# Two conv buffers and later gate matmuls in a recurrent branch, and modulation sums moved to another stage

## The chip, the cores and the metric

The kernel runs on one core of one Trainium2 chip. The metric is the device time of one execution in microseconds. A core has TensorE (PE, matrix multiplies into the PSUM banks), VectorE (DVE), ScalarE (ACT), GpSimd (POOL) and SyncE (SP, which here only issues transfers). Each engine runs its own list of instructions in order, and they wait for each other through semaphores.

## What is computed

Two blocks of a network on 1024 tokens of width 1024, in float32. The first block is a mixer of attention and a gated linear recurrence; the second takes its shift, scale and gate vectors ("modulation") from a small vector `c`. The parts that matter here:

```
proj = h @ w_in ; q, k, v, g_attn, x_lru, g_lru = split(proj)
xc = causal_depthwise_conv(x_lru, conv_w, conv_b)      # 4 taps
r  = sigmoid(xc_block @ w_r + b_r)                     # 8 blocks of 128
gi = sigmoid(xc_block @ w_i + b_i)
a  = exp(-8 * r * softplus(-lam))
h_t = a_t * h_{t-1} + sqrt(1 - a_t**2) * gi_t * xc_t
y_lru = h_t * silu(g_lru)
x = x + rmsnorm(concat(y_attn, y_lru) @ w_out)
...
mod = silu(c) @ w_ada_2 + b_ada_2                      # 6 x 1024 values, used from the second block on
```

## The kernel before

Activations lie feature-major: a tile is 128 features by 1024 tokens, and eight tiles make the width. Weights come as 255 slabs of 1024 x 128 (512 KB), in the order of their use, in two slots. For each slab SyncE issues one load (`load_slab`, L242) as soon as GpSimd has split the slab two places ahead. GpSimd splits it into a high part (L225, a cast) and a low part (L227, a subtraction), once TensorE has finished the slab two places ahead. `project` (L207 to L209) then multiplies it: for each of two chunks of 512 tokens, 8 inner tiles times 3 matmuls (high x high, high x low, low x high), 24 matmuls into one PSUM bank; chunk 0 goes to `proj_bank0`, chunk 1 to `proj_bank1`. A bank can be written again when ScalarE or VectorE has read it.

**Recurrent branch** (`lru_stage`, about 50 to 308 us of the trace, eight blocks n of 128 features, a loop on every engine). Each block has two slabs, one for x and one for the gate branch.
- TensorE: slab x, chunk 0 of the gate slab, six one-column matmuls that add up the modulation of the block before (`columns`, L499, shown as x12 since the profile counts the passes of a float32 matmul), chunk 1, and then, after a wait for the convolution, the four gate matmuls (L514, shown as x8).
- ScalarE: two silus (L542), two sigmoids (L546, L547), exp and tanh (L549, L550), the copy of the next block's x chunk 0 (L537), the square root (L554), the copy of chunk 1. Between kinds of functions it loads a table.
- VectorE: a copy of the block's gate weights (L598), the convolution (L599 and three times L602), the modulation's six values (L581), six of eight accumulations of modulation weights (L589, L591: `acc = w_ada[kt] * cond[kt] + acc`, 128 x 768), three steps of the recurrence (L609, L610, L612), the last two accumulations, the product with the root (L615), the scan (L617) and the product with silu (L620).
- SyncE: the loads of the next two slabs, and then eight loads of modulation weights (L490, 384 KB each, two buffers), each of which waits until VectorE has used the one two places ahead.

The convolution's output `lru_conv` is one buffer, read by the gate matmuls and by L612. The copy of the next x goes out only when the convolution has read the last.

**Attention** (about 308 to 1052 us): its first matmuls run at once, but its ScalarE part begins when all engines have ended the branch (`begin` waits for `stage_ended`). Its first copy of a chunk is L819.

**Output projection** (`out_project_stage`, about 1052 to 1230 us). VectorE first makes eight low parts of y (L1028). TensorE projects the last slabs of tile 0; then a loop of seven rounds f projects tile f+1, two slabs each. ScalarE squares and copies each tile (L1019, L1020), and VectorE adds the squares up (L1033), one instruction for each tile. The next stage (the norm, L277) begins when all engines have ended this one. SyncE's queue from slab 18 on is `rest_of_slabs`, a plain loop over pairs of slabs.

## Time and profile before

| | us |
|---|---|
| median of 3 runs | 3740.36 |
| lowest and highest run | 3737.33 and 3741.08 |
| span of the profiled execution | 3738.0 |
| TensorE busy | 3485.4 (93%) |
| VectorE busy | 1433.6 (38%) |
| ScalarE busy | 829.6 (22%) |
| GpSimd busy | 949.5 (25%) |

The profile gives no other time of the profiled execution than its span; it lies 2.4 us below the median run. Times in a timeline are counted from the start of the span. The busy time of a matmul overlaps with the next one's, so the distance from start to start is what a matmul costs. The granted clock of TensorE is given as a share of 2.4 GHz; 0.5 is its lower level.

### The profile page before, as it was taken

Reading aid. Unit: us, or ns where it says so; the run is one execution under the profiler, and the core shown is the slowest. Engines: PE = TensorE matmul, PEld = TensorE weight load, DVE = VectorE, ACT = ScalarE, POOL = GpSimd, SP = SyncE. Lnnn points to the kernel's source line nnn. Section 1 sums busy time; section 2 is a strip of 40 time slices with the busy share of each in tenths; the row PEclk is TensorE's granted clock in tenths of the full one; section 3 lists DMA queues with packets and bytes.
Section 4 is the critical chain, followed back from the end, with each engine's and each line's share of the span. In section 5 each row is a group of like instructions: output and inputs, shape, how many; then the busy total and the mean of one; then the engine's idle time right before and its main releaser. Section 6 shows DMA issues by size and latency. Waiting matters only on the chain.

```text
span 3738.0 us, 42270 instructions
## 1 busy us (share of the span) xinstructions
PE 3485.4 (93%) x16158; PEld 2816.6 (75%) x16158; DVE 1433.6 (38%) x1753; ACT 829.6 (22%) x1308; POOL 949.5 (25%) x514
## 2 busy tenths in 40 slices
PE   6888999999889798899999999979999989999999
PEld 5666777777668386677888888868878768888887
DVE  6774444444520557642012222321621543223231
ACT  3332232333320232232122222221110011101010
POOL 2222111111023131112322212224323323333332
PEclk9898999999889799989999999989999989999999
DMA  3432000000001211111121212232111211111112
GB/s 137 126 115 87 23 29 23 23 29 23 12 28 50 107 45 51 51 57 40 50 91 54 66 48 71 52 113 63 50 39 50 86 33 51 45 50 46 49 50 73
DMA packets 83681, 213.93 MB, mean 57 GB/s; under 512 B 7024, under 2 KB 33264, under 8 KB 83456
## 3 DMA queue, kind: packets, MB, share of 16 engines
q1 hardware_dynamic: 48176, 167.27, 14.2%
q10 hardware_dynamic: 35408, 45.24, 3.9%
q8 instruction: 77, 1.26, 0.1%
q14 instruction: 20, 0.16, 0.0%
HBM read 193.44 MB, written 19.04 MB: 57 GB/s over the span
## 4 chain that ended last, share of the span: by engine, by line
PE 81%; DVE 12%; ACT 2%; issue 2%; DMA 1%; PEld 0%; ACTq 0%; DVEq 0%; PEldq 0%; POOL 0%; SPq 0%; POOLq 0%
PE proj_bank L207 20%; PE proj_bank L209 19%; PE proj_bank L208 19%; PE aux_banks L719 3%; PE aux_banks L207 2%; PE aux_banks L209 2%; PE aux_banks L208 2%; PE aux_banks L785 1%; PE aux_banks L729 1%; PE aux_banks L1702 1%; PE aux_banks L514 1%; DVE lru_conv L602 1%; PE aux_banks L1385 1%; PE aux_banks L722 1%; DVE ada_acc L591 1%
## 5 line engine op out<-in xcount | busy, mean ns | idle before, releaser
L207 PE MATMUL proj_bank<-h_hi,slab_hi 128*128 128x512 f32 x2816 | 1131.5, 402 | 36.3 <-DVE h_lo L372 9.1
L208 PE MATMUL proj_bank<-h_lo,slab_hi 128*128 128x512 f32 x2816 | 1111.0, 395 | 0.0
L209 PE MATMUL proj_bank<-h_hi,slab_lo 128*128 128x512 f32 x2816 | 1110.8, 394 | 0.0
L225 POOL CAST slab_hi<-slab_raw 128x1024 fp32r<-128x1024 f32 x255 | 274.3, 1076 | 2745.9 <-PE proj_bank L209 2343.9
L227 POOL TENSOR_TENSOR slab_lo<-slab_raw,slab_hi 128x1024 fp32r<-128x1024 f32 x255 | 675.1, 2647 | 20.4
L207 PEld LDWEIGHTS proj_bank<-h_hi,slab_hi 128*128 128x128 f32 x2816 | 538.6, 191 | 160.1 <-issue 20.2
L209 PEld LDWEIGHTS proj_bank<-h_hi,slab_lo 128*128 128x128 f32 x2816 | 537.6, 191 | 116.3
L208 PEld LDWEIGHTS proj_bank<-h_lo,slab_hi 128*128 128x128 f32 x2816 | 538.7, 191 | 109.8 <-issue 2.2
L207 PE MATMUL proj_bank<-ffn_hi,slab_hi 128*128 128x512 f32 x512 | 199.2, 389 | 0.0
L208 PE MATMUL proj_bank<-ffn_lo,slab_hi 128*128 128x512 f32 x512 | 199.2, 389 | 0.0
L209 PE MATMUL proj_bank<-ffn_hi,slab_lo 128*128 128x512 f32 x512 | 199.2, 389 | 0.0
L2257 ACT ACTIVATE ffn_relu_squared<-proj_bank 128x512 f32<-128x512 f32 x64 | 38.4, 599 | 538.2 <-PE proj_bank L209 438.5
L2285 DVE SCALAR_TENSOR_TENSOR x<-proj_bank,mod,x 128x512 f32<-128x512 f32 x64 | 48.1, 751 | 276.2 <-PE proj_bank L209 276.2
L828 ACT ACTIVATE att_p<-aux_banks,small 128x256 f32<-128x256 f32 (+7 forms) x128 | 93.7, 737 | 215.2 <-DVE small L891 214.9
L2275 DVE SCALAR_TENSOR_TENSOR ffn_relu_squared<-ffn_relu_squared 128x1024 f32<-128x1024 f32 x32 | 51.8, 1619 | 219.3 <-ACT ffn_relu_squared L2257 219.3
L719 PE MATMUL aux_banks<-att_k,att_q 64*128 64x512 f32 (+3 forms) x320 | 132.2, 519 | 0.0
L889 DVE TENSOR_REDUCE small<-aux_banks 128x1 f32<-128x256 f32 (+7 forms) x128 | 96.1, 755 | 75.1 <-PE aux_banks L723 74.4
L207 PE MATMUL proj_bank<-y_hi,slab_hi 128*128 128x512 f32 x256 | 104.5, 408 | 10.5 <-DVE y_lo L1028 4.4
L208 PEld LDWEIGHTS proj_bank<-ffn_lo,slab_hi 128*128 128x128 f32 x512 | 96.1, 188 | 20.0
L209 PEld LDWEIGHTS proj_bank<-ffn_hi,slab_lo 128*128 128x128 f32 x512 | 96.1, 188 | 20.0
L207 PEld LDWEIGHTS proj_bank<-ffn_hi,slab_hi 128*128 128x128 f32 x512 | 96.1, 188 | 19.9
L208 PE MATMUL proj_bank<-y_lo,slab_hi 128*128 128x512 f32 x256 | 103.0, 402 | 0.0
(329 smaller groups left out, 4243.3 us busy)
## 6 DMA issues: line engine op xcount, KB each, us to landing
slab_raw<-wts SPq DMA_DIRECT2D x255, 512.0 KB, 3.5
ada_w<-ada_w SPq DMA_DIRECT2D x64, 384.0 KB, 3.1
ssd_decay_rows<-decay_sums ACTq DMA_DIRECT2D x16, 512.0 KB, 4.1
dil_rows<-dilated_out ACTq DMA_DIRECT2D x12, 520.0 KB, 8.0
x_first<-xT SPq DMA_DIRECT2D x4, 1024.0 KB, 9.5
x_again<-xT ACTq DMA_DIRECT2D x4, 1024.0 KB, 10.5
x_kept<-x ACTq DMA_DIRECT2D x8, 512.0 KB, 3.8
mix_kept<-ssd_mix ACTq DMA_DIRECT2D x8, 512.0 KB, 6.4
```

The costliest lines, as they stand in the source:

```text
L207: pe.matmul(bank, k.whi[:, slot, wk, :], hi[:, xk, cols], start=first and a == 0, stop=False)
L208: pe.matmul(bank, k.whi[:, slot, wk, :], lo[:, xk, cols], start=False, stop=False)
L209: mm = pe.matmul(bank, k.wlo[:, slot, wk, :], hi[:, xk, cols], start=False, stop=last and a == len(ks) - 1)
L225: pool.tensor_copy(k.whi[:, slot], k.raw[:, slot]).then_inc(k.s_hi, 1)
L227: pool.tensor_tensor(k.wlo[:, slot], k.raw[:, slot], k.whi[:, slot].bitcast(F32), ALU.subtract).then_inc(k.s_split, 1)
L514: mm = pe.matmul(k.aux[:, 2 * i + c, :], gw[:, i, :], xc[:, c * HALF:(c + 1) * HALF], start=True, stop=True)
L719: pe.matmul(score[:, 2 * c + a // HALF, 0:n], q, kt[rows, par, a:a + n], start=True, stop=True)
L828: act.activation(p[:, c, 0:keys], flat[:, c, 0:keys], ACT.Exp, bias=nmax[:, c:c + 1], scale=SCALE, accum_out=total[:, c:c + 1]).then_inc(s ...
L889: ins = dve.tensor_reduce(mx[:, c:c + 1], flat[:, c, 0:keys], AX, ALU.max)
L2257: act.activation(act2[:, f % 2, c * HALF:(c + 1) * HALF], k.bank[c][:], ACT.Copy).then_inc(s_read, 1)
L2275: dve.scalar_tensor_tensor(act2[:, f % 2], act2[:, f % 2], 0.0, act2[:, f % 2], ALU.max, ALU.mult).then_inc(s_sq, 1)
L2285: dve.scalar_tensor_tensor(xt, k.bank[c][:], k.mod[:, 40 + f:41 + f], xt, ALU.mult, ALU.add).then_inc(s_x2, 1)
```

## The change

- The branch is written out (no loops). `lru_conv` gets two buffers. On TensorE the gate matmuls of block n-1 stand between the x slab and the gate slab of block n. On ScalarE the copies of x(n) come first, then sigmoids, exp and tanh of n-1, the silus of n, the root of n-1. On VectorE the convolution of n comes ahead of the recurrence of n-1. The copy of the gate weights is gone; TensorE reads them where they were loaded.
- The modulation leaves the branch. Its loads, accumulations and columns are now in the output projection, one group of eight loads for each of the eight tiles: VectorE accumulates ahead of adding up the squares, and TensorE's `columns(f)` stand between the two slabs of round f, the last ones behind the loop. SyncE's queue has each group behind a pair of slabs (slabs 50 and 51 for the first), and the first loads wait until VectorE has begun the stage.

```diff
-def lru_stage(k, block, wts, gate_w, ada_w):
+def lru_stage(k, block, gate_w):
...
+    xc = k.at("lru_conv", k.W + 4.25, [P, 2, T])
...
     def _(pe):
...
-        with pe.Fori(0, LRU_BLOCKS) as n:
+        for n in range(LRU_BLOCKS):
             for s in range(2):
                 for c in range(2):
-                    pe.wait_ge(s_evac, n * 4 + (2 * s + c + 1))
-                    project(k, pe, n * 2 + (LRU_0 + s), s, c, k.bank[c][:], k.hhi, k.hlo, ready=h_ready)
-                    if s == 1 and c == 0:
-                        columns(n)
-            pe.wait_ge(s_conv, n + 2)
-            pe.wait_ge(s_sig, n + 1)
-            for i in range(2):
-                for c in range(2):
-                    mm = pe.matmul(k.aux[:, 2 * i + c, :], gw[:, i, :], xc[:, c * HALF:(c + 1) * HALF], start=True, stop=True)
-            mm.then_inc(s_gates, 1)
+                    pe.wait_ge(s_evac, 4 * n + 2 * s + c + 1)
+                    project(k, pe, LRU_0 + 2 * n + s, s, c, k.bank[c][:], k.hhi, k.hlo, ready=h_ready if n == 0 else None)
+                if s == 0 and n:
+                    gates(n - 1)
+        gates(LAST)
...
     def _(act):
...
+        for n in range(LRU_BLOCKS):
+            for c in range(2):
+                x_in(n, c)
+            if n:
+                decays(n - 1)
+            silu(n)
+            if n:
+                root(n - 1)
+        decays(LAST)
+        root(LAST)
...
     def _(dve):
...
+        for n in range(LRU_BLOCKS):
+            conv(n)
+            if n:
+                recurrence(n - 1)
+        recurrence(LAST)
...
 def out_project_stage(k, block):
...
                     project(k, pe, f * 2 + (OUT1_0 + 2 + s), s, c, k.bank[c][:], k.yhi, k.ylo,
                             [(i, i + KT * s) for i in range(KT)], s == 0, s == 1)
+                    if s == 0 and c == 1:
+                        columns(f)
+        columns(GROUPS - 1)
...
         with dve.Fori(0, KT) as f:
+            modulation(f)
             dve.wait_ge(s_added, f + 1)
             dve.wait_ge(s_evac, f * 2 + 4)
             dve.tensor_tensor(k.ssum, k.ssum, sq, ALU.add).then_inc(s_added, 1)
+            columns(f)
...
-def rest_of_slabs(k, block, wts):
+def rest_of_slabs(k, block, wts, ada_w):
...
+        with sp.Fori(0, KT) as n:
+            pair(n + first)
+            for kt in range(KT):
+                sp.wait_ge(k.s_ada_used, n * KT + (kt + 1))
+                sp.dma_start(k.adaw[:, kt % 2], ada_w[ds(n, 1), kt].rearrange("a p m -> (a p) m")).then_inc(k.s_ada[kt % 2], 16)
```

TensorE in the recurrent branch. Before, the end of a block of the loop (L207 to L209 are the gate slab, L514 the gate matmuls):

```order
L209 MATMUL proj_bank<-h_hi,slab_lo 128x512
L510 REGISTER_ALU
L511 REGISTER_ALU [waits lru_conv_made]
L514 MATMUL aux_banks<-lru_conv,gate_w 128x512 [waits lru_sigmoids]
L514 MATMUL aux_banks<-lru_conv,gate_w 128x512 x3
L503 REGISTER_ALU
L503 COMPARE_AND_BRANCH
```

TensorE after the change, the first gate matmuls (L206 to L208 are the x slab of block 1 ahead of them and its gate slab behind them, L492 the gate matmuls of block 0):

```order
L206 MATMUL proj_bank<-h_hi,slab_hi 128x512
L207 MATMUL proj_bank<-h_lo,slab_hi 128x512
L208 MATMUL proj_bank<-h_hi,slab_lo 128x512
L492 MATMUL aux_banks<-lru_conv,gate_w_all 128x512 [waits lru_conv_made,gate_w_loaded]
L492 MATMUL aux_banks<-lru_conv,gate_w_all 128x512 x3
L206 MATMUL proj_bank<-h_hi,slab_hi 128x512 [waits slab_split,lru_evacuated]
```

The gate matmuls ended their own block; they now stand one slab later, inside the next one.

ScalarE in the recurrent branch. Before, a block of the loop (L542 are the silus of n, L537 the copies of x of n+1):

```order
L542 ACT_TABLE_LOAD
L542 ACTIVATE y<-proj_bank 128x512
L541 REGISTER_ALU
L542 ISA [waits chunk_projected]
L542 ACTIVATE y<-proj_bank 128x512
L544 REGISTER_ALU
L546 ISA [waits lru_y_made,lru_gates]
L546 ACT_TABLE_LOAD
L546 ACTIVATE lru_r<-aux_banks,params 128x1024
```

ScalarE at the same place after the change (L524 are the copies of x of n, L535 to L539 sigmoids, exp and tanh of n-1, L529 the silus of n, L543 the root of n-1):

```order
L524 ACTIVATE lru_x<-proj_bank 128x512 [waits chunk_projected,lru_conv_made] x2
L535 ACT_TABLE_LOAD [waits lru_y_made]
L535 ACTIVATE lru_r<-aux_banks,params 128x1024 [waits lru_gates]
L536 ACTIVATE lru_i<-aux_banks,params 128x1024
L538 ACT_TABLE_LOAD
L538 ACTIVATE lru_a<-lru_r,small 128x1024 [waits lru_sigmoids]
L539 ACTIVATE lru_u<-lru_r,small 128x1024
L529 ACT_TABLE_LOAD
L529 ACTIVATE y<-proj_bank 128x512 [waits chunk_projected] x2
L543 ACT_TABLE_LOAD
L543 ACTIVATE lru_r<-lru_u 128x1024 [waits lru_m2]
```

The silus stood ahead of the sigmoids of their own block; they now stand behind the four activations of the block before, and the wait for the gates stands behind the table load.

VectorE in the output projection. Before, the loop holds one instruction for each tile:

```order
L1028 TENSOR_TENSOR y_lo<-y,y_hi 128x1024 [waits y_high] x7
L1029 MEMSET out_sum 128x1024
L1030 UNCONDITIONAL_BRANCH
L1030 ISA
L1032 ISA [waits out1_added]
L1033 TENSOR_TENSOR out_sum<-out_sum,out_squared 128x1024 [waits out1_evacuated]
```

VectorE, the end of the same loop after the change (L1020 is the last of eight accumulations, L1034 the sum of the squares, L1027 the six values that it reads from TensorE's columns):

```order
L1020 SCALAR_TENSOR_TENSOR ada_acc<-ada_w,small,ada_acc 128x768 [waits ada_loaded_1,ada_used]
L1022 REGISTER_ALU
L1032 REGISTER_ALU [waits ada_used]
L1033 ISA [waits out1_added]
L1034 TENSOR_TENSOR out_sum<-out_sum,out_squared 128x1024 [waits out1_evacuated]
L1027 ISA [waits ada_columns]
L1027 TENSOR_TENSOR mod<-aux_banks,params 128x6
```

Eight accumulations have come ahead of the sum, and the read of the columns behind it.

## Rows read from the trace of the kernel before

**Rows 1.** Table of stretches: length, engines' busy us, PEclk, DMA share, GB/s.

```profile
core 0: us, PE busy (x) PEld busy (x) DVE busy (x) ACT busy (x) POOL busy (x), PEclk, DMA share, GB/s
200.00:250.00 50.00, 43.74 (x162) 31.39 (x163) 35.69 (x29) 20.92 (x21) 11.28 (x5) 0.86 0.42 127
...
1150.00:1227.00 77.00, 77.00 (x341) 63.79 (x340) 3.68 (x3) 7.60 (x14) 26.89 (x14) 1.00 0.15 48
```

**Rows 2.** Table of waits, TensorE, 60 to 330 us: total, times, longest.

```profile
PE aux_banks L514 <- DVE lru_conv L602: 33.3, 7, 5.7
```

**Rows 3.** Timeline of TensorE in the branch: start, us, line, tile [idle before].

```profile
67.03 3.59 PE L514 MATMUL aux_banks<-lru_conv,gate_w 128*128 128x512 f32 x8
...
70.69 0.40 PE L208 MATMUL proj_bank<-h_lo,slab_hi 128*128 128x512 f32 x1
...
148.40 0.39 PE L207 MATMUL proj_bank<-h_hi,slab_hi 128*128 128x512 f32 x1
...
155.20 1.39 PE L499 MATMUL aux_banks<-small,ada_acc 128*128 128x1 f32 x12
...
156.78 0.40 PE L208 MATMUL proj_bank<-h_lo,slab_hi 128*128 128x512 f32 x1
...
167.90 5.99 PE L514 MATMUL aux_banks<-lru_conv,gate_w 128*128 128x512 f32 x8 [5.69 <-DVE lru_conv L602]
...
308.15 0.47 PE L207 MATMUL proj_bank<-h_hi,slab_hi 128*128 128x512 f32 x1 [0.41 <-PEq L701]
```

**Rows 4.** Groups by line, 30 to 330 us: busy us, mean ns | idle before.

```profile
L514 PE MATMUL aux_banks<-lru_conv,gate_w 128*128 128x512 f32 x64 | 45.1, 870 | 33.3 <-DVE lru_conv L602 33.3
L225 POOL CAST slab_hi<-slab_raw 128x1024 fp32r<-128x1024 f32 x17 | 23.2, 1362 | 222.1 <-DMA slab_raw<-wts 118.1 <-PE proj_bank L209 104.0
...
L542 ACT ACT_TABLE_LOAD x8 | 10.3, 1283 | 34.5 <-PE proj_bank L209 34.4
...
L542 ACT ACTIVATE y<-proj_bank 128x512 f32 (+1 forms) x16 | 9.6, 598 | 44.3 <-PE proj_bank L209 44.3
```

**Rows 5.** Timeline of ScalarE, VectorE and TensorE around the branch's last block.

```profile
190.88 2.29 DVE L617 TENSOR_TENSOR_SCAN lru_u<-lru_a,lru_i 128x1024 f32<-128x1024 f32 x1
...
307.79 1.12 ACT L546 ACTIVATE lru_r<-aux_banks,params 128x1024 f32<-128x1024 f32 x1 [9.06 <-PE aux_banks L514]
...
312.28 1.14 ACT L550 ACTIVATE lru_u<-lru_r,small 128x1024 f32<-128x1024 f32 x1
...
316.23 1.06 ACT L554 ACTIVATE lru_r<-lru_u 128x1024 f32<-128x1024 f32 x1 [1.51 <-DVE lru_u L610]
...
319.57 1.23 DVE L615 TENSOR_TENSOR lru_i<-lru_i,lru_r 128x1024 f32<-128x1024 f32 x1
...
324.10 2.95 DVE L620 TENSOR_TENSOR y<-lru_u,y 128x1024 f32 x1 [0.26 <-DVE lru_u L617]
...
328.25 0.79 PE L207 MATMUL proj_bank<-h_hi,slab_hi 128*128 128x512 f32 x1 [6.86 <-ACT att_q L819]
```

**Rows 6.** Instructions on one tile, GpSimd, 60 to 310 us: ns min/median/max.

```profile
L227 POOL TENSOR_TENSOR slab_lo<-slab_raw,slab_hi x15: 2950/3194/4249, 68.5 to 298.1; 128x1024 fp32r<-128x1024 f32 x15
```

**Rows 7.** Timeline of the output projection: its loop's start and its end.

```profile
1070.78 2.34 POOL L227 TENSOR_TENSOR slab_lo<-slab_raw,slab_hi 128x1024 fp32r<-128x1024 f32 x1
...
1073.18 0.50 PE L207 MATMUL proj_bank<-y_hi,slab_hi 128*128 128x512 f32 x1 [3.69 <-POOL slab_lo L227]
...
1229.89 2.87 PE L277 MATMUL aux_banks<-small,out_sum 128*128 128x1 f32 x16 [2.48 <-DVEq L191]
```

**Rows 8.** Timeline of VectorE, one block's accumulations of the modulation.

```profile
167.76 0.60 DVE L589 TENSOR_SCALAR ada_acc<-ada_w,small 128x768 f32<-128x768 f32 x1
...
171.36 1.02 DVE L591 SCALAR_TENSOR_TENSOR ada_acc<-ada_w,small,ada_acc 128x768 f32<-128x768 f32 x1 [1.94 <-DMA ada_w<-ada_w]
...
175.68 1.02 DVE L591 SCALAR_TENSOR_TENSOR ada_acc<-ada_w,small,ada_acc 128x768 f32<-128x768 f32 x1 [1.32 <-DMA ada_w<-ada_w]
...
177.66 1.02 DVE L591 SCALAR_TENSOR_TENSOR ada_acc<-ada_w,small,ada_acc 128x768 f32<-128x768 f32 x1 [0.96 <-DMA ada_w<-ada_w]
```

**Rows 9.** Instructions on the tile of the modulation weights, whole span: their landing.

```profile
DMA to landing us min/median/max: 2.8/3.1/6.5
```

More of the change, by code:

```diff
@@ L479, in lru_stage @@
     s_lam = k.sem("lambda_summed")
-    k.banks_read = (s_evac, 2 * LRU_SLABS + 2)
-    EV, AD = 2, 6
-    @block.sync
-    def _(sp):
-        with sp.Fori(0, LRU_BLOCKS) as n:
-            for s in range(2):
-                load_slab(k, sp, wts, n * 2 + (2 + s), s, True)
-            for kt in range(KT):
-                sp.wait_ge(s_ada_used, n * KT + (kt + 2))
-                sp.dma_start(adaw[:, kt % 2], ada_w[ds(n, 1), kt].rearrange("a p m -> (a p) m")).then_inc(s_ada[kt % 2], 16)
+    EV = 2
@@ L492, in _, with gates @@
+    k.banks_read = (s_evac, 2 * LRU_SLABS + EV)
+    LAST = LRU_BLOCKS - 1
     @block.tensor
     def _(pe):
-        def columns(n):
-            pe.wait_ge(s_ada_used, n * KT + 3)
-            pe.wait_ge(s_col, n * 2 + 1)
-            for j in range(AD):
-                mm = pe.matmul(k.aux[:, 4, j:j + 1], acc[:, j * P:(j + 1) * P], k.ones, start=True, stop=True)
-            mm.then_inc(s_col, 1)
+        def gates(n):
+            if n == 0:
+                pe.wait_ge(s_gw, 16)
+            pe.wait_ge(s_conv, n + 1)
+            if n:
+                pe.wait_ge(s_sig, n)
+            for i in range(2):
+                for c in range(2):
+                    mm = pe.matmul(k.aux[:, 2 * i + c, :], gw[:, n, i, :], xc[:, n % 2, c * HALF:(c + 1) * HALF], start=True, stop=True)
+            mm.then_inc(s_gates, 1)
@@ L516, in _ @@
+        gates(LAST)
         end(k, pe)
         def last_sums():
-            columns(LRU_BLOCKS)
             pe.wait_ge(k.s_vec, 1)
@@ L546, in rest @@
[L546 to L552 removed]
+            if n:
+                act.wait_ge(s_y, n)
@@ L990, in out_project_stage, with columns @@
     k.ssum = k.at("out1_sum", k.W + 36, [P, T])
-    s_evac, s_added = k.sem("out1_evacuated"), k.sem("out1_added")
+    adaw, acc = k.adaw, k.at("ada_acc", k.W + 46, [P, ADA_COLS])
+    s_evac, s_added, s_col = k.sem("out1_evacuated"), k.sem("out1_added"), k.sem("ada_columns")
+    AD = ADA_COLS // P
+    GROUPS = KT
     @block.tensor
     def _(pe):
+        def columns(n):
+            pe.wait_ge(k.s_ada_used, n * KT + (KT + 2))
+            for j in range(AD):
+                mm = pe.matmul(k.aux[:, 4, j:j + 1], acc[:, j * P:(j + 1) * P], k.ones, start=True, stop=True)
+            mm.then_inc(s_col, 1)
         begin(k, pe)
```

132 lines of the change are left out of this document (58 added, 74 removed).

## The prediction

> **What bounds the kernel now.** I looked first at the table of stretches, to see which engine fills each stage. In the output projection TensorE is busy for the whole stretch and its granted clock is full; in the recurrent branch it is busy for 43.7 of 50 us with a granted clock of 0.86, while VectorE is busy for 35.7 us [rows 1]. So the branch is the one of the two touched stages in which TensorE is kept waiting, and the table of waits says by whom: from 60 to 330 us TensorE waited 33.3 us, in seven pieces, for the last step of the convolution (L602) [rows 2]. The timeline shows the shape of a block: the gate matmuls (L514) stand right behind the second slab, so they wait for a chain that begins only when the recurrence of the block before has left VectorE. They then run long: 5.99 us behind a wait, against 3.59 us in block 0, where there was none [rows 3]. That is the granted clock: behind the idle time the matmuls go at the lower of the two levels, 1.2 GHz, for a while.
>
> The Trainium skill says the same, in "TensorE: Matmul & The Clock Gate", section "HAM oscillation — how this bites in real kernels": a wait in each round lets the clock fall, and each round pays for it again. The trace agrees (5.99 against 3.59 us); a sum of the waits alone would leave out some 16 us, which is the first rival below.
>
> **Recurrent branch, removed and moved.** Unit prices first. 30 projection matmuls stand between the starts at 148.40 and 155.20, so one takes 0.2267 us and a slab (48 of them) 10.88 us. The gate matmuls at full clock: 67.03 to 70.69 holds them and one projection matmul, so 3.66 - 0.23 = 3.43 us. The columns of the modulation (L499): 155.20 to 156.78 holds them and one matmul, so 1.35 us [rows 3]. Now the stretch from the first gates (67.03) to the first matmul of the attention (308.15): 241.1 us. After the change, block 0 reaches that point without columns, at 67.03 - 1.35 = 65.68, and what is left are 14 slabs and 8 sets of gates: 14 x 10.88 + 8 x 3.43 = 179.8 us, up to 245.4. That is **62.7 us less**. As a cross-check, by parts: 33.3 us of waits, 45.1 - 8 x 3.59 = 16.4 us of slow gates [rows 2 to 4], 8 x 1.35 = 10.8 us of columns, and 2.2 us of slow matmuls behind the gates.
>
> This holds only if nothing else sets the pace of 25.2 us a block. ScalarE has the tightest place: silu of chunk 0 now stands behind the four activations of the block before, and it frees the bank that the next x slab needs 10.9 us after the gates end. From the last block, written out in straight code already: the sigmoids begin at 307.79, the tanh ends at 313.42, 5.6 us; a table load 1.28 and the silu 0.6 make 7.5 us [rows 4, 5]. 3.3 us are left. VectorE: the convolution needs only its own block's x, which is there 24 us before the gates ask for the result. The recurrence: silu of chunk 1 ends 11.5 us after the gates, table load and root 2.3, and 5.0 to 7.5 us for product, scan and y (worked out below), so 19 to 21.5 us, before the next x is complete at 22. GpSimd needs 1.4 + 3.2 = 4.6 us a slab, 5.6 with the longest subtraction here (4.25), of 10.9 [rows 4, 6]. SyncE has only slabs left in its queue, so these come earlier than before.
>
> **Start of the attention.** ScalarE may take the attention's first chunk only when VectorE has ended the branch. TensorE waits 6.9 us for that (L819). Before: sigmoids at 307.79, root ends at 317.29, 9.5 us; then two accumulations (L591) stand in front of the product at 319.57; y ends at 327.05, TensorE goes on at 328.25 [rows 5]. The accumulations go. Product, scan and y took 4.53 + 2.95 = 7.5 us here, beside GpSimd; with the short scan of 2.29 and a y as long as the product they take 1.23 + 2.29 + 0.26 + 1.23 = 5.0. So 9.5 + 5.0 to 7.5 + 1.2 = 15.7 to 18.2 us; I take 17.1, for GpSimd's subtraction falls into this place as before. TensorE resumes at 245.4 + 17.1 = 262.5, against 328.25. With the 62.7 us that makes **65.8 us**, 64.6 to 67.1.
>
> **Output projection, added.** The loads, sums and columns of the modulation come here, one group a tile. Three terms:
> - Columns: 7 in the loop x 1.35 = **9.4 us** on TensorE, which has no free time there [rows 1]; 8.8 if the slow matmul behind them is spared.
> - The first slab of the loop: TensorE waits 3.69 us for GpSimd's split (L227, 2.34 us, VectorE mostly idle) [rows 7]. VectorE now accumulates at that time, and in the branch, where it did, the subtraction took 3.19 us at the median and 4.25 at most [rows 6]: **0.9 us**, 0 to 1.9. The Trainium skill ("GPSIMD Engine Reference", section "Specifications") says that GpSimd shares its SBUF interfaces with VectorE and contends with instructions that read two SBUF inputs, as the accumulation does; the medians agree.
> - The end. A group in the branch went 167.76 (first piece), 171.36 (third), 175.68 (fifth), 177.66 (sixth) [rows 8]. Carried on at 4.32 us a pair: 3.60 + 2 x 4.32 + 1.98 + 1.02 = 15.2 us. Within the loop a group may take from one tile's columns to the next's, 21.8 + 1.35 = 23.1 us, of which 1.65 go for columns and their read: 15.2 < 21.4, so 6 us are left and TensorE doesn't wait. The last group has only the second slab beside it. Counted from the middle of the last round it ends at 1.65 + 15.2 = 16.9 us, while the matmuls end at 12.2; then come the columns at the lower clock (up to 2.5 us), their read and the end of the stage, so the next stage begins at 18.9 to 20.0. Before, it began 10.9 + 2.5 us after that point [rows 7]; with the seventh columns already counted, 14.75. **4.7 us**, 4.1 to 5.3.
>
> SyncE's queue: slabs now stand behind eight loads of the modulation that each wait for VectorE. The last of them is issued some 11 us into the group, so a slab's load is issued up to 9 us later than now. But the split can't begin before the slab two places ahead has been projected, another 10 us later, and the longest landing of a modulation load is 6.5 us [rows 9]; so this costs nothing. The first eight loads wait until VectorE begins the stage, and the first group (from about 1064 to 1079) is through before its columns are wanted at 1086.
>
> **Sum.** 65.8 - 9.4 - 0.9 - 4.7 = 50.8 us. The profiled execution spans 3738.0 us, 2.4 less than the median of 3740.4; against the median: 3740.4 - 50.8 = **3689.6**. Its own range goes from 3685 to 3693 by the bounds above, and some 4 us more on either side for clock levels that fall differently in the later stages: 3681 to 3697.
>
> **Rivals.**
> 1. The gates stay slow: TensorE's clock doesn't hold, although it doesn't wait. Then only waits and columns go, 16.4 us less: 3706. For it: the gates carry twice the time of a projection matmul, and only block 0 shows eight of them at the full clock. Against: 77 us of unbroken work at 1.00 [rows 1]. Chance 0.05.
> 2. ScalarE or VectorE paces the branch. If the 3.3 us in front of silu are used up and 3 us more, each of seven blocks loses 3 us: +21, 3711. For it: y and the convolution stretch to 3 us beside GpSimd. Against: the counts above. Chance 0.08.
> 3. The loads pace the output projection mildly, a group taking 24.5 us instead of 21.4: 7 x 3.1 = 22, and 9 at the end, with slow matmuls behind the waits: 3725. Chance 0.06.
> 4. The other side: every modulation load takes 6.5 us, the longest in the branch, instead of 3.1 [rows 9], because it queues with slabs and other traffic. Then the first pair and the two next take 3.4 us more each: 25.4 us a group. A round takes 27.1 + 0.2 = 27.3 instead of 23.1 us, 7 x 4.2 = 29.4; the last group ends 10.3 us later; and eight waits leave 2.4 us of slow matmuls each (5.99 - 3.59), 19.2. 65.8 - 0.9 - 9.4 - 29.4 - 15.0 - 19.2 = -8.1: 3748.5, **slower**. It begins to cost at a landing of 5.2 us and turns the sum at about 6.2. Against: the median of 3.1 was taken with the same slabs in the same queue within 34 us, in a stage with more traffic a microsecond (127 GB/s [rows 1]). Chance 0.04.
> 5. The change does not do what it says: silent waits (a semaphore counted too low or a tile shared) keep gates where they were. Then the branch gains only columns and accumulations, about 20 us, and the projection costs 15: 3735. Chance 0.02.
>
> **Numbers.** The forecast has 0.75. A range of 3681 to 3711 holds it, rival 1 and half of rival 2, 0.84. A measurement of this kernel tells 0.2% (7.5 us) from no change. Faster by more: forecast and rivals 1 to 3, 0.94; within: rival 5, 0.02; slower: rival 4, 0.04.
>
> **What would show it.** Right: no wait of TensorE for the convolution between 60 and 245 us; gate matmuls of about 3.6 us in every block; 25.2 us from gates to gates; attention from about 245 us; in the output projection 23.1 us a tile, and one wait of 4 to 5 us for the accumulation, ahead of the last columns. Wrong: TensorE waiting for a silu (rival 2), for the accumulation or a split slab in the loop (3, 4), gates of 5 to 6 us without a wait (1).

## The result

| | kernel before | kernel after |
|---|---|---|
| median, us | 3738.85 (4 runs) | 3699.38 (4 runs) |
| lowest and highest run, us | 3737.22 and 3741.08 | 3692.71 and 3703.97 |
| span of the profiled execution, us | 3738.0 | 3698.0 |

The changed kernel takes 0.9892 of the time before, with an interval of 0.9878 to 0.9905. That is 1.1% less, about 10 us above the predicted time of 3689.6: inside the stated range of 3681 to 3711, but 2.4 us outside the 3681 to 3697 that the forecast had by itself. Between the two profiled spans lie 40.0 us; the sum had 50.8.

Four points of the trace are enough to see where the 40 us come from: the first matmul of the attention, the moment at which TensorE goes on after its wait for the attention's first copy, the normalisation behind the attention's head groups (the matmuls over `att_o_squared` that end it), and the first matmul of the norm behind the output projection.

| us from the start of the span | before | forecast | after |
|---|---|---|---|
| attention's first matmul | 308.15 | 245.4 | 246.54 |
| TensorE goes on | 328.25 | 262.5 | 270.41 |
| last sums of the attention begin | 1042.20 | | 983.35 |
| norm behind the output projection begins | 1229.89 | | 1189.87 |
| from there to the end of the span | 2508.1 | unchanged | 2508.1 |

So the branch was right to 1.1 us, the start of the attention 7.9 us late (those 1.1 among them), the attention itself 1.0 us shorter (712.9 against 714.0), and the stretch with the output projection grew by 18.8 us (206.5 against 187.7) where 15.0 were forecast: 50.8 - 7.9 + 1.0 - 3.8 = 40.1.

### The profile page after: what moved, and what is told of

The parts are those of the page before. It is cut to its first block, busy times and chain, and to the rows that moved or that the text cites. A ratio compares the mean times of both kernels' runs of the same rounds, so it can differ in the third digit from the quotient of the medians.

```text
span 3698.0 us, 41916 instructions
## 1 busy us (share of the span) xinstructions
PE 3464.7 (94%) x16146; PEld 2809.8 (76%) x16146; DVE 1438.5 (39%) x1743; ACT 830.5 (22%) x1308; POOL 930.2 (25%) x514
## 4 chain that ended last, share of the span: by engine, by line
PE 85%; DVE 9%; ACT 2%; issue 1%; DMA 1%; ACTq 0%; PEld 0%; PEldq 0%; DVEq 0%; POOL 0%; SPq 0%; POOLq 0%
PE proj_bank L206 21%; PE proj_bank L207 21%; PE proj_bank L208 21%; PE aux_banks L687 3%; PE aux_banks L206 2%; PE aux_banks L207 2%; PE aux_banks L208 2%; PE aux_banks L753 1%; PE aux_banks L697 1%; PE aux_banks L1717 1%; PE aux_banks L1400 1%; PE aux_banks L690 1%; PE aux_banks L1741 1%; PE aux_banks L492 1%; DMA ada_w<-ada_w 1%
## 5 line engine op out<-in xcount | busy, mean ns | idle before, releaser
L206 PE MATMUL proj_bank<-h_hi,slab_hi 128*128 128x512 f32 x2816 | 1128.4, 401 | 42.7 <-ACT att_q L787 12.4
L207 PE MATMUL proj_bank<-h_lo,slab_hi 128*128 128x512 f32 x2816 | 1108.6, 394 | 0.0
L208 PE MATMUL proj_bank<-h_hi,slab_lo 128*128 128x512 f32 x2816 | 1108.4, 394 | 0.0
L226 POOL TENSOR_TENSOR slab_lo<-slab_raw,slab_hi 128x1024 fp32r<-128x1024 f32 x255 | 660.1, 2589 | 20.4
L206 PEld LDWEIGHTS proj_bank<-h_hi,slab_hi 128*128 128x128 f32 x2816 | 537.1, 191 | 165.6 <-issue 19.7
L208 PEld LDWEIGHTS proj_bank<-h_hi,slab_lo 128*128 128x128 f32 x2816 | 536.2, 190 | 115.3
L207 PEld LDWEIGHTS proj_bank<-h_lo,slab_hi 128*128 128x128 f32 x2816 | 537.5, 191 | 109.3 <-issue 2.2
L206 PE MATMUL proj_bank<-ffn_hi,slab_hi 128*128 128x512 f32 x512 | 199.2, 389 | 0.0
L207 PE MATMUL proj_bank<-ffn_lo,slab_hi 128*128 128x512 f32 x512 | 199.2, 389 | 0.0
L208 PE MATMUL proj_bank<-ffn_hi,slab_lo 128*128 128x512 f32 x512 | 199.2, 389 | 0.0
L206 PE MATMUL proj_bank<-y_hi,slab_hi 128*128 128x512 f32 x256 | 106.0, 414 | 11.2 <-POOL slab_lo L226 4.4
L207 PEld LDWEIGHTS proj_bank<-ffn_lo,slab_hi 128*128 128x128 f32 x512 | 96.1, 188 | 20.0
L206 PEld LDWEIGHTS proj_bank<-ffn_hi,slab_hi 128*128 128x128 f32 x512 | 96.1, 188 | 19.9
L208 PEld LDWEIGHTS proj_bank<-ffn_hi,slab_lo 128*128 128x128 f32 x512 | 96.1, 188 | 19.9
L207 PE MATMUL proj_bank<-y_lo,slab_hi 128*128 128x512 f32 x256 | 103.2, 403 | 0.0
```

The source lines that it names most:

```text
L206: pe.matmul(bank, k.whi[:, slot, wk, :], hi[:, xk, cols], start=first and a == 0, stop=False)
L207: pe.matmul(bank, k.whi[:, slot, wk, :], lo[:, xk, cols], start=False, stop=False)
L208: mm = pe.matmul(bank, k.wlo[:, slot, wk, :], hi[:, xk, cols], start=False, stop=last and a == len(ks) - 1)
L226: pool.tensor_tensor(k.wlo[:, slot], k.raw[:, slot], k.whi[:, slot].bitcast(F32), ALU.subtract).then_inc(k.s_split, 1)
```

## The profile after

The table of stretches of the changed kernel: us, busy us and instructions of each engine, granted clock of TensorE (1.00 is 2.4 GHz), DMA share, GB/s. The second line is the stretch of [rows 1].

```profile
60.00:240.00 180.00, 180.00 (x745) 139.74 (x744) 106.04 (x70) 88.58 (x90) 50.09 (x28) 1.00 0.13 44
200.00:250.00 50.00, 49.59 (x197) 36.75 (x197) 30.83 (x21) 25.20 (x25) 14.26 (x8) 1.00 0.12 43
```

TensorE is busy for all of the 180 us at the full clock; before it was busy for 43.7 of 50 us at 0.86 [rows 1]. The table of waits of TensorE from 60 to 330 us names no convolution any more, where [rows 2] had 33.3 us in seven waits. What is at its head is the start of the attention, and it is longer than the 6.86 us of [rows 5]:

```profile
PE proj_bank L206 <- ACT att_q L787: 12.4, 1, 12.4
```

The timeline of TensorE in the branch (start, us, line, tile). These are the gate matmuls of blocks 5, 6 and 7; [rows 3] had 5.99 us for a set behind a wait and 3.59 for one without:

```profile
203.01 3.59 PE L492 MATMUL aux_banks<-lru_conv,gate_w_all 128*128 128x512 f32 x8
...
228.21 3.59 PE L492 MATMUL aux_banks<-lru_conv,gate_w_all 128*128 128x512 f32 x8
...
242.54 3.60 PE L492 MATMUL aux_banks<-lru_conv,gate_w_all 128*128 128x512 f32 x8
```

All eight sets take 3.59 or 3.60 us and stand 25.2 us apart, except the last, which has only the gate slab between it and the one before: 14.3 us. That spacing is the key to the next rows, the timeline of ScalarE at the end of the branch (in square brackets the idle time before, and what ended it):

```profile
244.65 1.06 ACT L543 ACTIVATE lru_r<-lru_u 128x1024 f32<-128x1024 f32 x1
251.08 1.28 ACT L535 ACT_TABLE_LOAD   x1 [5.38 <-DVE y L584]
252.38 1.12 ACT L535 ACTIVATE lru_r<-aux_banks,params 128x1024 f32<-128x1024 f32 x1
...
263.31 1.06 ACT L543 ACTIVATE lru_r<-lru_u 128x1024 f32<-128x1024 f32 x1 [4.00 <-DVE lru_u L577]
...
269.76 1.09 ACT L787 ACTIVATE att_q<-proj_bank 128x512 f32<-128x512 f32 x2 [3.91 <-DVEq L190]
```

The last gates end at about 246.1 us, but the last sigmoids start at 252.38. They write into `lru_r`, which the recurrence of block 6 still reads: its root is only made at 244.65, and its y is ready at 251.0. In every other block the copies of the next x and its whole slab lie in between; behind the last block there is nothing. VectorE and GpSimd show a second delay in the same place (both timelines, same columns):

```profile
258.03 1.96 DVE L576 TENSOR_TENSOR lru_r<-lru_a 128x1024 f32<-128x1024 f32 x1 [7.03 <-ACT lru_u L539]
260.03 3.25 DVE L577 SCALAR_TENSOR_TENSOR lru_u<-lru_r,lru_u 128x1024 f32<-128x1024 f32 x1
...
264.46 1.23 DVE L580 TENSOR_TENSOR lru_i<-lru_i,lru_r 128x1024 f32<-128x1024 f32 x1
```

```profile
257.88 1.04 POOL L224 CAST slab_hi<-slab_raw 128x1024 fp32r<-128x1024 f32 x1 [11.54 <-PE proj_bank L208]
258.99 3.19 POOL L226 TENSOR_TENSOR slab_lo<-slab_raw,slab_hi 128x1024 fp32r<-128x1024 f32 x1
```

L576 and L577 take 1.22 us each when GpSimd does not start first. Here L576 starts 0.15 us behind GpSimd's cast and ends 1.07 us behind the cast's end; L577 starts within the subtraction and ends 1.1 us behind its end. And the subtraction, which started while L576 was under way, took 3.19 us instead of 2.40 (the median of its 15 instances in the branch after). So whichever of the two starts first keeps the other out until it is through, and the other then takes its usual time, or 0.1 to 0.2 us less (1.07 and 1.10 us instead of 1.22, 2.19 instead of 2.40). The Trainium skill has this in "SBUF — State Buffer", section "SBUF: two separate sides": one pair of ports is locked for a whole instruction by the engine that starts first, where VectorE reads two SBUF inputs, as L576 and L577 do. The trace agrees in both directions, to the 0.2 us just given.

At the end of the output projection the timelines of TensorE and VectorE show one wait, ahead of the last columns, as forecast, but 8.95 us long instead of 4 to 5:

```profile
1165.31 1.39 PE L970 MATMUL aux_banks<-small,ada_acc 128*128 128x1 f32 x12
...
1186.70 2.72 PE L970 MATMUL aux_banks<-small,ada_acc 128*128 128x1 f32 x12 [8.95 <-DVE ada_acc L1020]
1189.87 2.29 PE L276 MATMUL aux_banks<-small,out_sum 128*128 128x1 f32 x10 [0.45 <-DVEq L190]
```

```profile
1167.75 1.83 DVE L1018 TENSOR_SCALAR ada_acc<-ada_w,small 128x768 f32<-128x768 f32 x1 [0.70 <-DMA ada_w<-ada_w]
...
1172.90 1.02 DVE L1020 SCALAR_TENSOR_TENSOR ada_acc<-ada_w,small,ada_acc 128x768 f32<-128x768 f32 x1 [2.27 <-DMA ada_w<-ada_w]
...
1179.40 4.05 DVE L1020 SCALAR_TENSOR_TENSOR ada_acc<-ada_w,small,ada_acc 128x768 f32<-128x768 f32 x2 [1.22 <-DMA ada_w<-ada_w]
1185.62 1.02 DVE L1020 SCALAR_TENSOR_TENSOR ada_acc<-ada_w,small,ada_acc 128x768 f32<-128x768 f32 x1 [2.17 <-DMA ada_w<-ada_w]
```

GpSimd in the same stretch:

```profile
1166.76 2.40 POOL L226 TENSOR_TENSOR slab_lo<-slab_raw,slab_hi 128x1024 fp32r<-128x1024 f32 x1
...
1179.16 2.34 POOL L226 TENSOR_TENSOR slab_lo<-slab_raw,slab_hi 128x1024 fp32r<-128x1024 f32 x1
```

The last group goes from 1167.75 to 1186.64, 18.9 us, where 15.2 were forecast from [rows 8]. Its first piece and its sixth were caught by GpSimd's subtractions: 1.83 us instead of 0.60, and 4.05 us for two instead of 2.04. And a piece that ends late frees its buffer late, so that the load behind it is late too. In the loop nothing waits: the columns stand 23.16 us apart, and from 1020 to 1160 us TensorE is busy throughout at the full clock:

```profile
1020.00:1160.00 140.00, 140.00 (x654) 117.03 (x653) 73.73 (x60) 13.04 (x24) 42.77 (x24) 1.00 0.55 175
```

## Experiments

The theory to test: the branch gains because the convolution is ready before TensorE asks for it, which needs both parts of the change; the start of the attention is late because of the one set of gate buffers; the end of the output projection is late because the loads' landing and GpSimd's split pace the last group. The kernels ran four and four on two chips, the first four of them (two sets, one group early, and the two without modulation) beside a median of 3736.8 us for the kernel before, the others beside 3739.1, so ratios are compared and not times.

**Two sets of gate buffers.** The rest of the changed kernel is as it is.

```diff
+    names = ("lru_r", "lru_i", "lru_a", "lru_u")
+    sets = [[k.at(n, k.W + 12.25 + 4 * i, [P, T]) for i, n in enumerate(names)],
+            [k.at(n + "_2", k.Y + 4 + 4 * i, [P, T]) for i, n in enumerate(names)]]
...
         def decays(n):
             act.wait_ge(s_gates, n + 1)
-            if n:
-                act.wait_ge(s_y, n)
+            r, g, a, u = sets[n % 2]
+            if n > 1:
+                act.wait_ge(s_y, n - 1)
```

> The changed kernel with a second set of the four tiles lru_r, lru_i, lru_a, lru_u, used by odd blocks; nothing is left out. Theory (one set of tiles holds the start of the attention): in the changed kernel the last sigmoids began 6.2 us after the last gate matmuls, because ScalarE waited for y of block 6. With two sets they begin with the gates' end (about 246.2), VectorE ends the branch by 261 to 263, TensorE resumes at 262 to 264 instead of 270.4, and the whole is 6 to 8 us shorter than the changed kernel's 3699.4: 3691 to 3693. Rival (the late start comes from VectorE's steps beside GpSimd's split, which took 1.96 and 3.25 us instead of 1.23): the sigmoids are early and the resumption still later than 268, the whole within 2 us of the changed kernel's.

Timeline of ScalarE and of TensorE: the last sigmoids start at 247.01, right behind the root of block 6 and a table load, and TensorE goes on at 264.91.

```profile
247.01 1.12 ACT L538 ACTIVATE lru_r<-aux_banks,params 128x1024 f32<-128x1024 f32 x1
```

```profile
264.91 0.79 PE L206 MATMUL proj_bank<-h_hi,slab_hi 128*128 128x512 f32 x1 [6.92 <-ACT att_q L792]
```

The wait is 6.92 instead of 12.39 us: 5.5 us of the missing 7.9 hang on the shared set. But the median was 3694.26 us, a ratio of 0.9889 (0.9871 to 0.9907), the same as the change's own. The 5.5 us were there at 265 us and gone at 983.35 us, the start of the attention's last sums, which is to the hundredth where it is in the kernel after. How they went is told below. The expected whole, 6 to 8 us shorter than the change, is not shown.

**One of eight groups early.** The group of the last tile is loaded and accumulated in the branch, one piece a block behind the convolution; its columns lie in TensorE's wait ahead of the attention.

```diff
         for n in range(LRU_BLOCKS):
             conv(n)
+            half = (EARLY + 1) // 2
+            for p in range(n * EARLY, n * EARLY + half):
+                piece(p)
...
-        with pe.Fori(0, KT - 1) as f:
+        def tile(f, more):
...
-        columns(GROUPS - 1)
+
+        with pe.Fori(0, KT - EARLY) as f:
+            tile(f, True)
```

> The changed kernel with the eighth group of modulation weights moved back into the branch: one load and one accumulation in each block, into an accumulator of its own, its columns behind the attention's first two chunks, where TensorE waits anyway. The output projection keeps seven groups, with columns in its seven rounds and none behind the loop. Nothing is left out. Theory (the last group has only half a round beside it): the wait of 9.0 us and the columns of 2.7 us go, the next stage begins 2.5 us after the last matmul, 9 to 10 us are saved: 3689 to 3690. Rival (the accumulation costs the branch as much, because VectorE's steps there get longer): the attention starts more than 3 us later than 246.5, and less than 6 us are saved.

The wait for the accumulation was gone; the norm followed the last slab by 2.55 us, as before the change [rows 7]. From the start of the output projection's loop to the norm it took 167.7 us (1019.44 to 1187.11), after the change 176.0 (1013.85 to 1189.87), before it 156.7 [rows 7]: the eleven us that are left are the seven columns, 9.6, and 1.2 of lower clock in the loop's first slab. The profiled execution, the slowest of the four, was 5.0 us longer than that of the change all the same: its attention took 4.9 us more (717.8), and the stages from the norm on 7.8 us more (2515.9 against 2508.1), with nothing changed there. The ratio, 0.9874 (0.9855 to 0.9893), can't be told from the change's 0.9892.

**The change without the modulation.** Loads, accumulations and columns are left out.

> The changed kernel without the modulation: its loads, accumulations and columns are left out, and the modulation is the bias alone, so the output differs. This measures what the modulation costs in the output projection. Theory (it costs only what the trace shows there: seven columns 9.6 us, the end 9.7 us, 0.7 us at the first split slab): 20 us less than the changed kernel, 3679 to 3680. Rival (its loads also slow other stages, by traffic or by clock levels): over 25 us less, under 3675.

The modulation is the bias alone here. The stretch with the output projection took 187.7 us, to a tenth what it took before the change, so that the modulation's price there is 18.8 us. Its parts: up to the loop's first slab 0.5 us less than before the change, although the wait for that slab was 0.7 longer (4.42 against 3.68 us); columns 7 x 1.37 = 9.6; and the end, 24.56 us from the seventh columns to the norm (1165.31 to 1189.87) in the place of 14.8 (1.37 for those columns, a slab of 10.88, and the 2.5 of [rows 7]), 9.8. The median was 3684.58 us, 0.9869 (0.9848 to 0.989). By the ratios that is only 8.6 us less than the change, where 20 were expected, and the intervals overlap; the profiled execution, of 3674.3, was the shortest of its four, and 23.7 us shorter than that of the change. The 18.8 us are thus shown in the stretch, and not in the kernel's time.

**The kernel before without the modulation, and the new order without the move.** The first leaves the same work out of the kernel before. The second, shown as a diff to the kernel after, has the written-out branch and the two conv buffers, with the accumulations spread over its blocks.

```diff
-            columns(n)
-            modulation(n, range(KT - 2))
             dve.wait_ge(s_au, n + 1)
...
-            modulation(n, range(KT - 2, KT))
```

> The kernel before without the modulation: its loads, accumulations and columns are left out of the branch, and the modulation is the bias alone, so the output differs; order and buffers are those of before. This parts the gain of the move from that of the new order. Theory (both are needed): columns (10.8 us) and accumulations go, but the convolution still stands behind the recurrence, a chain of 21 to 26 us after the gates against TensorE's 21.8 us, so waits of 1 to 4 us a block remain, and slow gates behind them: 3700 to 3715, with 7 waits of TensorE for the convolution, 7 to 28 us in total. Rival (the move alone gives the gain, the order nothing): no waits for the convolution, and a time within 4 us of the changed kernel without the modulation, about 3680.

```diff
         for n in range(LRU_BLOCKS):
             conv(n)
             if n:
-                recurrence(n - 1)
+                column_read(n - 1)
+                pieces(n, range(3))
+                recurrence(n - 1, range(3, 5), range(5, KT))
```

> The new order and the two conv buffers, with the whole modulation left in the branch as before (eight loads and accumulations a block, three behind the convolution, two ahead of the product, three behind y, the columns behind the next x slab), and the output projection of before. Nothing is left out. Theory A (the order is what gives the gain, the move is worth little): TensorE still paces the branch, 25.2 + 1.4 us a block; the attention's first matmul starts at 257 to 260, TensorE waits for nothing in the branch, and the output projection loses its 18.8 us: 3690 to 3695. Theory B (both are needed, since VectorE has 13.6 us of the recurrence and 8 us of accumulations in a block, and GpSimd's two splits stretch its steps by 2 us each): VectorE or ScalarE behind it paces the branch at 27 to 30 us a block, the first matmul starts at 262 to 285, with waits of TensorE for ScalarE or VectorE in most blocks.

The tables of waits of TensorE, 60 to 330 us, of the first and of the second:

```profile
PE aux_banks L509 <- DVE lru_conv L594: 17.4, 7, 2.5
```

```profile
PE aux_banks L505 <- DVE ada_acc L598: 21.4, 7, 3.8
```

And the stretch from 60 to 240 us of each:

```profile
60.00:240.00 180.00, 165.10 (x653) 123.80 (x653) 100.34 (x69) 79.21 (x81) 65.68 (x26) 0.97 0.12 38
```

```profile
60.00:240.00 180.00, 164.63 (x657) 124.87 (x656) 131.90 (x104) 66.35 (x68) 45.38 (x23) 0.92 0.38 128
```

Without the modulation the old order still waits seven times for the convolution, 2.5 us each, and the attention's first matmul comes at 270.36 us: 37.8 of the branch's 61.6 us. The order brings the other 23.8; where TensorE goes on, 17.8 of them are left (288.17 against 270.41), since the new order pays for its shared set there. The median of this kernel was 3697.85 us, a ratio of 0.9899 (0.988 to 0.9917), shorter than the 3700 to 3715 expected. Its time can't be told from that of the changed kernel with the modulation, and its interval overlaps that of the changed kernel without it (0.9869): what the order brings when the modulation is gone is seen in the branch, and not shown in the time. But with the modulation left in the branch the order brings only 9.0 us there (299.16): the seven waits are now for the accumulation, and the gates behind them are at the lower clock again (5.38 us). In that kernel VectorE paces the branch: it is busy for 131.90 of 180 us, and stands waiting some 1.9 us at a time for a load in between, with the next convolution queued behind it. The attention's first matmul comes later than either theory allowed (285 at most). The ratio was 0.9972 (0.9961 to 0.9984), a quarter of the gain of the change. Neither part alone makes the branch free of waits; for the order this holds for the whole modulation, placed as it was here.

**Loads only twice.** 62 of 64 loads are left out; every piece accumulates what the first two brought. Matmuls, accumulations and columns all stay.

```diff
-                dve.wait_ge(k.s_ada[kt % 2], n * 64 + 16 * (kt // 2 + 1))
+                dve.wait_ge(k.s_ada[kt % 2], 16)
```

> The changed kernel in which only the first two loads of modulation weights are made and all 64 accumulations read these two buffers, so the modulation and the output differ; all accumulations and columns are there. This parts the last group's length (18.9 us in the changed kernel, 15.2 forecast) into loads and VectorE's work. Theory (the loads' landing sets the pace, and GpSimd's splits add 1 to 2 us each): the group shrinks to 8 to 12 us, all of it under the 10.9 us of the last slab; TensorE waits at most 1.5 us for the last accumulation, and the output projection from the attention's last statistics to the norm's first matmul takes 187.7 + 9.6 = 197 to 199 us instead of 206.5. Rival (VectorE beside GpSimd is the cause): the group stays over 14 us and TensorE waits 3 us or more.

The last group took 9.7 us and TensorE did not wait for it (timeline of VectorE, then of TensorE):

```profile
1168.06 2.32 DVE L1018 TENSOR_SCALAR ada_acc<-ada_w,small 128x768 f32<-128x768 f32 x1 [0.21 <-issue]
1170.41 7.34 DVE L1020 SCALAR_TENSOR_TENSOR ada_acc<-ada_w,small,ada_acc 128x768 f32<-128x768 f32 x7
```

```profile
1178.39 1.39 PE L970 MATMUL aux_banks<-small,ada_acc 128*128 128x1 f32 x12
1181.11 2.12 PE L276 MATMUL aux_banks<-small,out_sum 128*128 128x1 f32 x16 [1.32 <-DVEq L190]
```

So without the loads, two buffers deep, the last group is 9.2 of its 18.9 us shorter. The second meeting with GpSimd is gone with them, since the group is through before the next subtraction. Even here the first piece takes 2.32 us, since GpSimd's subtraction (1167.56, 2.40 us) had started before it. The stretch was 10.1 us shorter than after the change. There is one run only, at 3691.62 us, too few for a verdict on the time.

What one meeting costs can be read from the kernel with two sets. There the sixth piece of the last group began 0.07 us ahead of the subtraction, where after the change it began 0.24 us behind it (timelines of VectorE and GpSimd):

```profile
1178.85 1.02 DVE L1025 SCALAR_TENSOR_TENSOR ada_acc<-ada_w,small,ada_acc 128x768 f32<-128x768 f32 x1 [1.26 <-DMA ada_w<-ada_w]
```

```profile
1178.92 3.14 POOL L226 TENSOR_TENSOR slab_lo<-slab_raw,slab_hi 128x1024 fp32r<-128x1024 f32 x1
```

The piece took its 1.02 us and the subtraction had to wait; the seventh piece lost 1.1 us. The group took 16.4 us instead of 18.9, and TensorE waited 6.52 us for it instead of 8.95.

**The gates at their old place.** Everything of the change stays, but the gate matmuls stand behind their own block's gate slab again, ScalarE has the order of before, and VectorE makes the next convolution between the third step of the recurrence and its product.

```diff
-                if s == 0 and n:
-                    gates(n - 1)
-        gates(LAST)
+            gates(n)
...
             v.settle(dve, dve.tensor_tensor(g[:], g[:], xc[:, n % 2], ALU.mult))
+            if n < LAST:
+                conv(n + 1)
             dve.wait_ge(s_mult, n + 1)
```

> The changed kernel with the gate matmuls back behind their own gate slab and ScalarE in the order of before (silus, sigmoids, exp, tanh, copy of the next x, root, copy); on VectorE the convolution of the next block stands between the first half of the recurrence and the product with the root. Nothing is left out. Theory (what counts is that the convolution stands ahead of the product, scan and y; a slab later for the gates isn't needed, and it is what costs 6 us at the end of the branch, where no slab stands between): no wait of TensorE for the convolution, the attention's first matmul at 246.5, the last sigmoids with the gates' end, TensorE resumes at 262 to 266 instead of 270.4, about 6 us less in the branch and its end. Rival (the slab between is needed): waits for the convolution of 1 us and more a block remain, the first matmul starts after 254.

No wait in the branch; the attention's first matmul comes at 245.74, and TensorE goes on at 263.45, 7.0 us sooner than after the change. So the later gate matmuls, which give the change its name, are not what it needs: a convolution that doesn't wait for the recurrence's end is enough, and the last block then pays nothing for a shared set. The measured ratio, 0.9885 (0.9868 to 0.9903), again shows nothing of the 7 us.

**Four groups early, and two sets.** The first two experiments together, with four of eight groups in the branch, four pieces a block: VectorE is busy there for 106.04 of 180 us, 14.8 of the 25.2 us of a block, and four pieces take 4.1.

> The changed kernel with two sets of recurrence tiles and with four of the eight modulation groups in the branch: four loads and accumulations a block, four accumulators in the room of y's first half, their columns all in TensorE's wait behind the attention's first two chunks. The output projection keeps four groups in its first four rounds, none behind the loop. Nothing is left out. Theory: the branch stays at 25.2 us a block (first matmul of the attention at 246.5), TensorE resumes at 264 to 268, the output projection takes 187.7 + 4 x 1.4 + 0.7 = 194 us from the attention's last statistics to the norm instead of 206.5; 12 us less there and 3 to 6 us less at the attention's start: 15 to 18 us less than the changed kernel, if the attention's own clock levels don't differ: 3681 to 3685. Rival (VectorE is full): waits of TensorE in the branch, its end after 250, and less than 8 us gained.

The branch stays without a wait: the same stretch from 60 to 240 us has VectorE busy for 139.40 us instead of 106.04, and TensorE's clock is full.

```profile
60.00:240.00 180.00, 180.00 (x746) 139.70 (x745) 139.40 (x99) 88.58 (x90) 54.36 (x28) 1.00 0.31 106
```

TensorE goes on at 264.89, of its wait only 1.47 us are left (the 24 early columns fill 5.66 us of it), and the stretch with the output projection takes 192.65 us instead of 206.5. The median was 3677.22 us, a ratio of 0.9836 (0.9819 to 0.9853): better than both kernels, by 62 us against before and, taking the ratios, by 21 us against the change, where 15 to 18 were expected.

## Why the gains at 265 us didn't reach the end

Between the point at which TensorE goes on and the attention's last sums all kernels run the same instructions. It took them from 708.5 to 721.4 us: 712.9 after the change, 718.4 with two sets, 721.4 with the gates in place, 711.2 with four groups early. The starts of GpSimd's casts, one for each slab, show that the difference comes in steps. Between the change and the kernel with the gates in place there are six of 1 to 4 us up to 833 us, all for the change, and one of 5.7 us the other way behind 897 us; between the steps two kernels keep their distance to 0.05 us, over up to 145 us. Two stretches of the same work (between the casts of the same slabs), first in the kernel after, then in the one with the gates in place:

```profile
451.69:555.34 103.65, 103.48 (x544) 81.72 (x543) 49.03 (x96) 34.16 (x63) 16.91 (x10) 1.00 0.08 26
555.34:580.39 25.05, 22.31 (x112) 18.18 (x111) 6.51 (x18) 7.75 (x15) 3.39 (x3) 0.86 0.07 23
```

```profile
446.67:550.32 103.65, 103.48 (x544) 81.72 (x543) 49.02 (x96) 34.17 (x63) 16.92 (x10) 1.00 0.08 26
550.32:579.04 28.72, 25.19 (x112) 20.30 (x111) 6.51 (x18) 7.74 (x15) 3.39 (x3) 0.76 0.06 20
```

The first stretch is the same to the hundredth. In the second TensorE stands idle for 2.7 and 3.5 us (two pauses ahead of a group of heads, of 1.7 and 1.0 us in the one and 2.1 and 1.5 in the other, for which the trace names no other engine), its clock falls to 1.2 GHz in both, and comes back sooner in the one than in the other: 0.86 against 0.76 on average, and 3.7 us more, 0.8 of them pause. The work that VectorE, ScalarE and GpSimd do there is the same to a hundredth. At three of the six places TensorE isn't idle at all. Here is the one ahead of 833 us, the same work in both kernels again:

```profile
814.21:833.47 19.26, 19.26 (x112) 16.23 (x110) 6.51 (x18) 7.74 (x15) 3.39 (x2) 1.00 0.09 28
```

```profile
818.24:840.68 22.44, 22.44 (x112) 18.76 (x111) 6.51 (x18) 7.75 (x15) 3.40 (x3) 0.85 0.07 24
```

In the second kernel the clock fell while TensorE was busy with one-column matmuls, those over `att_o_squared` (16 records at 829.83 us), and the first projection matmuls behind them took 0.63 us instead of 0.40; in the first kernel the same matmuls left it at the full level. The other two such places, ahead of 410 and 663 us, have 1.00 against 0.92.

What each such place costs thus differs with the same instructions in it, so some microseconds won ahead of the attention come out of it larger, smaller or not at all. The runs of one kernel scatter over as much: the four of the change from 3692.71 to 3703.97 us. The kernel without the modulation, whose attention begins within 0.03 us of the change's, stayed within 0.2 us of it up to 897 us and was 4.5 us ahead at the last sums (978.87 against 983.35). That is why two sets and the gates in place are shown to do what they should at 265 us, and not shown to gain. What decides whether the clock falls, and how long it stays low, is left open; no run varied a pause or one of these matmuls alone.

## Why the prediction was right, and where it was wrong

- **Branch, 62.7 us: right** (61.6). 14 slabs and 8 sets of gates at the full clock; of the 1.1 us, 0.4 lie ahead of the first gates (76.97 against 76.56) and 0.4 are the idle time ahead of the attention's first matmul that stands in the last row of [rows 3] too. The slow gates were rightly counted with the waits: a sum of waits alone (rival 1) would have left out 16 us.
- **ScalarE's and VectorE's slack: right.** No wait for a silu; rival 2 did not come.
- **Start of the attention, 15.7 to 18.2 us from its first matmul to the point at which TensorE goes on: wrong; it took 23.9.** The step that failed is "sigmoids at 307.79, root ends at 317.29, 9.5 us": it took over a duration of the kernel before, and with it, unsaid, that the sigmoids start as the gates end. In the new order the recurrence of block 6 is then still to come, and both use one set of buffers. The sigmoids came 5.8 us behind that first matmul, where the sum has them start, the root's end took 2.5 us more, with VectorE kept out by GpSimd, and product, scan and y took 1.5 less than the 6.4 that the value taken had in it: 6.8 us. Two sets, which remove the first cause, gave back 5.5.
- **Columns, 9.4 us: right** (9.6). **First slab, 0.9:** the wait grew by 0.7 as forecast, but 1.2 us were won back ahead of it, where the granted clock was 0.77 (before: 0.72) between the attention's last sums and the loop: -0.5 in all.
- **End of the output projection, 4.7 us: mis-sized; 9.8 on the same count**, a wait of 8.95 us in the place of 4 to 5. The 15.2 us of a group were worked out from six accumulations of a block of the branch that met no subtraction of GpSimd (a later block of the same trace has a first piece of 2.62 us, at 268.18); in the new place a subtraction starts with every slab, and two met this group. They made it 1.2 and 2.0 us longer, and the loads behind came later for that. For this stage the prediction looked at the pair in one direction only, GpSimd made slower by VectorE. The rest is 0.8 us up to the group's start and 0.7 behind its end.
- **SyncE's queue at no cost: right.** From 1014 us on TensorE waited for no slab. Rivals 3 and 4 did not come, and neither did 1 and 5 (all eight sets of gates moved, at 3.6 us): the landing of a modulation load was 3.1 us at the median and 6.7 at most (64 loads), as in [rows 9]; a single late one is taken up by the 6 us of slack in a round.
- **Sum:** 50.8 - 6.8 - 1.1 - 3.8 + 1.0 = 40.1 against 40.0 in the profiled spans. The stages behind were unchanged to a tenth. That the attention and the stages behind agree so well is partly luck: with the same instructions they took 708.5 to 721.4 us and 2506.5 to 2515.9 us in the other kernels.
- **Range.** The way the gain comes was forecast rightly, but its size, 50.8 us, was 11 us too large, by two terms that lay outside their own bounds. The measured 3699.4 us lies in the stated range only because that was widened upwards for rivals 1 and 2, which did not come.

## What to carry to other kernels

Before a step is moved ahead of another's end, list for the last round, where nothing follows that would hide it, which buffers both use; that round has its own critical path, and its durations can't be taken from the old order. Price work on VectorE beside GpSimd in both directions, by whole instructions: the one that starts second waits for the first to end. Work that must leave a stage fits best where an engine's own count shows slack: half of the modulation cost nothing in the branch once the order was right, while all of it cost 18.8 us in a stage in which TensorE has no free time.

## What the runs showed of the hardware

- VectorE and GpSimd lock each other out for whole instructions: an accumulation of 0.60 us took 1.83 and 2.32 us, a subtraction on GpSimd of 2.40 us took 3.19, each up to the other's end and then its usual time, to 0.2 us.
- Identical stages of some 715 us differ by up to 13 us between kernels, mostly in steps of 1 to 4 us, at places where TensorE's granted clock falls to the lower level in one kernel and not, or for a shorter time, in the other: the stretch of 25.05 us at 0.86, with pauses of 1 to 2 us, took 28.72 at 0.76, and one of 19.26 us at 1.00, without any pause, took 22.44 at 0.85.
- A short wait costs more than its length: the old order without the modulation had seven waits of 2.5 us, 17.4 together, and the attention began 24.6 us later than in the kernel with the gates in place, which had none (270.36 against 245.74); behind two of the waits the gate matmuls took 5.39 us instead of 3.59.
